# Expert weights of three token blocks added into DRAM by GpSimd's indirect transfers, one-hot products for the fourth

## The reference, cut to what matters

```python
sc = einsum('thcd,hcnd->thcn', q, sub_keys)        # 8 heads, 2 halves, 128 keys each
s1, i1 = top_k(sc[:, :, 0], 16); s2, i2 = top_k(sc[:, :, 1], 16)
top_s, pos = top_k(all 256 sums s1 + s2, 16)       # idx = i1 * 128 + i2 at pos
g = softmax(top_s)                                 # per token and head, over 16
act = gelu(u_tab[idx] @ hb); out = (g * act) @ v_tab[idx]
```

## Time and profile before

| | us |
|---|---|
| runs | 3403.22, 3407.58, 3408.45 (median 3407.58) |
| profiled execution | 3407.45, its span 3405.7 |
| experts: first steps to first one-hot product | 725 to 1292.7 |
| one-hot products | 1292.7 to 1600 |
| SP's first load back of `gd` | 1630.3 |
| GpSimd busy | 439.6 of 3405.7 |

### The profile page before, as it was taken

One profiled execution on the slowest core, in us unless ns is written; L12 is line 12 of the kernel. 1 busy time (PEld: TensorE's weight loads), 2 busy tenths in 40 slices (PEclk: granted clock), 3 DMA queues, 4 the chain that ended last, 5 costly groups with the idle time before them and its releaser, 6 DMA issues.

```text
span 3405.7 us, 37836 instructions
## 1 busy us (share of the span) xinstructions
PE 3253.8 (96%) x14880; PEld 2663.0 (78%) x14880; DVE 1926.9 (57%) x3440; ACT 1232.9 (36%) x1770; POOL 439.6 (13%) x516
## 2 busy tenths in 40 slices
PE   7989999999999999999999999999999977899999
PEld 6767777778888878888788888887888855688887
DVE  5654444567777776665555555555444567544443
ACT  4663444432222235555322222223222233532221
POOL 0000000020000007885000000002000344030000
PEclk9999999899999999999999999999999986799999
DMA  4323111324443445778855555542333310022331
GB/s 139 92 87 100 56 56 56 126 93 129 143 137 126 129 135 158 191 197 204 295 194 195 194 198 198 198 148 75 99 99 99 115 62 13 13 74 99 99 99 62
DMA packets 271199, 424.21 MB, mean 125 GB/s; under 512 B 144816, under 2 KB 148400, under 8 KB 271024
## 3 DMA queue, kind: packets, MB, share of 16 engines
q1 hardware_dynamic: 271024, 421.80, 39.1%
HBM read 348.87 MB, written 72.88 MB: 124 GB/s over the span
## 4 chain that ended last, share of the span: by engine, by line
PE 86%; DVE 7%; ACT 5%; POOL 1%; issue 1%; DMA 1%; SPq 0%; POOLq 0%; ACTq 0%
PE pb L539 27%; PE pb L540 27%; PE pb L541 27%; PE pb L819 3%; ACT scr L1051 2%; DVE S L1486 1%; DVE ST L1494 1%; ACT S L1054 1%; DVE ST L1486 1%; DVE whl L1486 1%; ACT L1051 1%; POOL pad L2018 0%; POOL pad L2015 0%; ACT whl L1054 0%; DVE scr L1494 0%
## 5 line engine op out<-in xcount | busy, mean ns | idle before, releaser
L539 PE MATMUL pb<-H,whl 128*128 128x512 f32 x2416 | 992.2, 411 | 24.2 <-DVE whl L1486 11.6
L540 PE MATMUL pb<-H,whl 128*128 128x512 f32 x2416 | 953.7, 395 | 0.0
L541 PE MATMUL pb<-H,whl 128*128 128x512 f32 x2416 | 953.1, 394 | 0.0
L1486 DVE TENSOR_TENSOR whl<-raw,whl 128x1024 fp32r<-128x1024 f32 (+4 forms) x550 | 649.6, 1195 | 436.8 <-ACT whl L1054 434.7
L1054 ACT ACTIVATE whl<-raw 128x1024 fp32r<-128x1024 f32 (+4 forms) x550 | 543.9, 1003 | 466.2 <-PE pb L541 465.9
L539 PE MATMUL pb<-S,whl 128*128 128x512 f32 (+1 forms) x1716 | 670.2, 391 | 18.8 <-DVE whl L1486 11.7
L540 PE MATMUL pb<-S,whl 128*128 128x512 f32 (+1 forms) x1716 | 667.9, 389 | 0.0
L541 PE MATMUL pb<-S,whl 128*128 128x512 f32 (+1 forms) x1716 | 667.6, 389 | 0.0
L539 PEld LDWEIGHTS pb<-H,whl 128*128 128x128 f32 x2416 | 462.1, 191 | 117.5 <-DVE whl L1486 13.7
L541 PEld LDWEIGHTS pb<-H,whl 128*128 128x128 f32 x2416 | 460.8, 191 | 99.1
L540 PEld LDWEIGHTS pb<-H,whl 128*128 128x128 f32 x2416 | 462.5, 191 | 85.4 <-issue 3.4
(11 more groups left out here) (186 smaller groups left out, 2739.5 us busy)
## 6 DMA issues: line engine op xcount, KB each, us to landing
raw<-in_pu SPq DMA_DIRECT2D x128, 512.0 KB, 3.9
raw<-in_pv SPq DMA_DIRECT2D x128, 512.0 KB, 4.5
raw<-in_w_in SPq DMA_DIRECT2D x72, 512.0 KB, 3.7
ad<-scr SPq DMA_DIRECT2D x128, 256.0 KB, 4.2
gd<-ST SPq DMA_DIRECT2D x8, 4096.0 KB, 21.3
GA<-gd SPq DMA_DIRECT2D x60, 512.0 KB, 4.6
GA<-ad SPq DMA_DIRECT2D x60, 512.0 KB, 6.3
raw<-in_wg SPq DMA_DIRECT2D x44, 512.0 KB, 3.3
```

Of the source, the lines that this page charges most:

```text
L539: e.matmul(o, lh, h, start=start, stop=False, skip_group_check=True)
L540: e.matmul(o, lh, l, start=False, stop=False, skip_group_check=True)
L541: return e.matmul(o, ll, h, start=False, stop=stop, skip_group_check=True)
L1486: return e.tensor_tensor(o, x, y, op)
```

## The change

- Each head is worked one ahead: the query projections (`pq`) and scores (`sk`) of head h+1 stand on TensorE while DVE makes the lists of head h; both have two banks. The low part of a query is a step of its own (`lo`), and on ACT the split of a projection's unit comes behind the query's copy. A head has 64 `u` steps between its parts instead of 80.
- The softmax is made per head: a subtract after `best`, an Exp on ACT of 64 columns, and in `share` the sum, reciprocal, product, and the address (i1 * 128 + i2) * 512 + token.
- SP clears `gd` in the attention with 32 transfers of 1 MB. GpSimd, for token blocks 0 to 2, issues 16 indirect transfers per block and head, each of which adds one number per partition to `gd` in DRAM; a block's transfers of head h wait for those of head h-1.
- Block 3 alone goes through transposes (3), `rows`, `g` (128) and `put` (32). GpSimd builds no one-hot rows. SP's stores take 32 tokens each.
- In the first FFN `sum_of` stands after the second `gate` product.

```diff
@@ peer_order: the order of the choice @@
+    out.append(("pq", 0, 0))
+    u(16)
+    out.append(("sk", 0, 0))
+    out.append(("sk", 0, 1))
     for h in range(8):
         for c in range(2):
-            if (h, c) != (0, 1):
-                out.append(("pq", h, c))
-            u(16)
-            out.append(("sk", h, c))
+            if h < 7:
+                out.append(("pq", h + 1, c))
+            out.append(("top", h, c))
+            if h < 7:
+                out.append(("lo", h + 1, c))
+            u(8 + 8 * c)
+        for c, step in enumerate(("cand", "best")):
+            out.append((step, h))
+            if h < 7:
+                out.append(("sk", h + 1, c))
             u(8)
-        for step in (("cand", h), ("best", h), ("pick", h, 0), ("pick", h, 1)):
-            out.append(step)
+        for c in range(2):
+            out.append(("pick", h, c))
             u(8)
-    out.append(("soft",))
-    u(20)
-    for z in range(3):
-        out.append(("over", z))
-        u(6)
-    left = 8 * (128 - s // 8 - 9)
+        out.append(("share", h))
+        u(8)
+    out.append(("over",))
+    u(8)
+    left = 8 * (116 - s // 8)
     for q in range(3):
         out.append(("rows", q))
-    for q in range(128):
-        if q + 3 < 128:
+    for q in range(32):
+        if q + 3 < 32:
             out.append(("rows", q + 3))
         for k in range(4 * q, 4 * q + 4):
             out.append(("g", k))
             if k % 4 == 3 and q:
                 out.append(("put", q - 1))
-            u((k + 1) * left // 512 - k * left // 512)
-    out.append(("put", 127))
-    u(8 * (124 - s // 8))
+            u((k + 1) * left // 128 - k * left // 128)
+    out.append(("put", 31))
+    u(64)
     out.append(("ga",))
...
@@ build: names @@
+        pq_bank, sk_bank = (2, 6), (3, 7)
+        place = place_t[:, :].rearrange("p (b h k) -> p b h k", b=4, h=8)
...
+        g_rows = gd.rearrange("i p t -> (i p t)").unsqueeze(1)
...
+        def share_of(h):
+            return ST_t[:, 3264 + 64 * (h % 2):3328 + 64 * (h % 2)]
...
@@ tensor: experts @@
-                            q.wait_ge(dve, ("pq", n - 1))
-                            linear(j, bank[2], Hh, Hl, h2, ("pq", n))
+                            q.wait_ge(dve, ("pq", n - 2))
+                            linear(j, bank[pq_bank[c]], Hh, Hl, h2, ("pq", n))
...
-                        q.wait_ge(dve, ("top", n - 1) if n else ("bra", 7))
+                        q.wait_ge(dve, ("top", n - 2) if n > 1 else ("bra", 7))
+                        if n == 1:
+                            q.wait_ge(act, ("rstd", "2"))
...
-                        z = step[1]
-                        if z == 0:
-                            q.wait_ge(act, ("rstd", "2"))
-                        q.wait_ge(dve, "soft")
-                        if z:
-                            q.wait_ge(dve, ("over", z - 1))
-                        for b in range(4):
-                            c = slice(128 * b, 128 * b + 128)
-                            last = e.transpose(bank[6][:, c], (I1, I2, TS)[z][:, c], ident)
-                        last.then_inc(prod.up(("over", z)), 1)
+                        q.wait_ge(dve, ("shared", 7))
+                        for z in range(3):
+                            c = slice(128 * z, 128 * z + 128)
+                            last = e.transpose(bank[6][:, c], (I1, I2, TS)[z][:, 384:512], ident)
+                        last.then_inc(prod.up("over"), 1)
...
-                        elif k == 0:
-                            q.wait_ge(dve, ("top", 15))
-                        if n % 4 < 3:
-                            q.wait_ge(pool, ("hot1", k))
-                        q.wait_ge(dve, ("hot2", k))
-                        last = e.matmul(b[:, c], hot2[n % 4][:, c], hot1[n % 4][:, c], start=True, stop=True, skip_group_check=True)
+                        q.wait_ge(dve, ("hot", k))
+                        last = e.matmul(bank[gbank[n % 4]][:, c], hot2[n % 4][:, c], hot1[n % 4][:, c], start=True, stop=True,
+                                        skip_group_check=True)
...
@@ tensor: ffn @@
-                            two(j, (bank[0], bank[2]), Hh, Hl, hx, (("gate", tag, 0), ("up", tag, 0)), tag)
+                            two(j, (bank[0], bank[2]), Hh, Hl, hx, (("gate", tag, 0), ("up", tag, 0)), tag if tag == "5" else None)
                             continue
                         linear(j, bank[i % 2], Hh, Hl, hx, ("gate", tag, i))
+                        if i == 1 and tag == "3":
+                            sum_of(tag)
...
@@ scalar: experts @@
-                        weights("w_pq", n)
                         if n == 0:
+                            weights("w_pq", 0)
...
-                        copy(qh[c], bank[2]).then_inc(act.up(("pq_hi", n)), 1)
+                        copy(qh[c], bank[pq_bank[c]]).then_inc(act.up(("pq_hi", n)), 1)
+                        weights("w_pq", n)
...
-                    elif what == "soft":
-                        q.wait_ge(dve, "shifted")
-                        run(ACT.Exp, TS, TS).then_inc(act.up("shares"), 1)
...
+                    elif what == "best":
+                        h = step[1]
+                        q.wait_ge(dve, ("shifted", h))
+                        run(ACT.Exp, share_of(h), share_of(h)).then_inc(act.up(("shares", h)), 1)
...
@@ vector: experts @@
+                        weights("sk", 2 * step[1] + step[2])
+                    elif what == "top":
                         h, c = step[1:]
                         n = 2 * h + c
-                        weights("sk", n)
                         q.wait_ge(prod, ("sk", n))
                         for b in range(4):
-                            best16(vals[:, c, b, :], idxu[:, c, b, :], bank[3][:, 128 * b:128 * b + 128], sc2, ("top", n))
+                            best16(vals[:, c, b, :], idxu[:, c, b, :], bank[sk_bank[c]][:, 128 * b:128 * b + 128], sc2, ("top", n))
+                    elif what == "lo":
+                        h, c = step[1:]
+                        n = 2 * h + c
+                        q.wait_ge(act, ("pq_hi", n))
+                        tt(ql[c], bank[pq_bank[c]], f(qh[c]), ALU.subtract).then_inc(dve.up(("pq", n)), 1)
...
+                        soft = share_of(h).rearrange("p (b k) -> p b k", b=4)
+                        tt(soft, TSv[:, :, h, :], TSv[:, :, h, 0:1].to_broadcast([128, 4, 16]), ALU.subtract).then_inc(
+                            dve.up(("shifted", h)), 1)
...
-                    elif what == "soft":
...
+                    elif what == "share":
+                        h = step[1]
+                        top, soft = TSv[:, :, h, :], share_of(h).rearrange("p (b k) -> p b k", b=4)
+                        total, at_ = sm_t[:, 0:4], ST[:, 3392:3456].rearrange("p (b k) -> p b k", b=4)
+                        then(stt(at_, I1v[:, :, h, :], 128.0, I2v[:, :, h, :], ALU.mult, ALU.add))
+                        then(stt(at_, at_, 512.0, tok, ALU.mult, ALU.add))
+                        then(e.tensor_copy(place[:, :, h, :], at_))
+                        q.wait_ge(act, ("shares", h))
+                        then(e.tensor_reduce(total, soft, AX_X, ALU.add))
+                        then(e.reciprocal(total, total))
+                        then(tt(top, soft, total.unsqueeze(2).to_broadcast([128, 4, 16]), ALU.mult), ("shared", h))
                     elif what == "over":
...
                     elif what == "rows":
...
-                        if n % 4 == 3:
-                            tt(o1.rearrange("p (u i) -> p u i", u=4), iota.unsqueeze(1).to_broadcast([128, 4, 128]),
-                               I1[:, 4 * n:4 * n + 4].unsqueeze(2).to_broadcast([128, 4, 128]), ALU.is_equal)
+                        tt(o1.rearrange("p (u i) -> p u i", u=4), iota.unsqueeze(1).to_broadcast([128, 4, 128]),
+                           I1t[:, 4 * n:4 * n + 4].unsqueeze(2).to_broadcast([128, 4, 128]), ALU.is_equal)
                         for k in range(4 * n, 4 * n + 4):
                             c = slice(128 * (k % 4), 128 * (k % 4) + 128)
-                            ts(o2[:, c], iota, I2[:, k:k + 1], ALU.is_equal, TS[:, k:k + 1], ALU.mult).then_inc(
-                                dve.up(("hot2", k)), 1)
+                            ts(o2[:, c], iota, I2t[:, k:k + 1], ALU.is_equal, TSt[:, k:k + 1], ALU.mult).then_inc(
+                                dve.up(("hot", k)), 1)
...
@@ gpsimd @@
-            for n in range(128):
-                if n % 4 < 3:
-                    q.wait_ge(dve, ("over", 2))
-                    if n > 3:
-                        q.wait_ge(prod, ("g", n - 4))
-                    for k in range(4 * n, 4 * n + 4):
-                        c = slice(128 * (k % 4), 128 * (k % 4) + 128)
-                        e.tensor_scalar(hot1[n % 4][:, c], iota, I1[:, k:k + 1], None, ALU.is_equal).then_inc(
-                            pool.up(("hot1", k)), 1)
+            q.wait_ge(zeroed, "cleared")
```

(54 more changed lines are left out.)

40 lines of the change are left out of this document (15 added, 25 removed).

## The result

| | before | after |
|---|---|---|
| median of the runs, us | 3406.59 (3403.22 to 3408.45, 4 runs) | 3327.52 (3326.48 to 3328.51, 4 runs) |
| span of the profiled execution | 3405.7 | 3326.3 |

The ratio is 0.9769 (95% interval 0.9752 to 0.9786): 79 us less. The forecast was 3339 with 3303 to 3410.

The account below looks back on a forecast made before the run. TensorE, busy 96% of the span, was taken as the bound, so work and waits removed from it come off the time. 3407.45 - 88.3 - 1.0 - 6.6 - 8.4 + 23.5 + 10.6 + 2 = 3339 us, range 3303 to 3410.

Parts of the forecast that it names:

- One-hot products, -88.3: One-hot part on TensorE: 384 of 512 products go, at 0.230 us each, saving 88.3 us.
- Softmax, -6.6: The one softmax over all heads goes: TensorE's 4.4 us idle and 2.2 us of slow clock are saved.
- the transposes: Before the one-hot products: nine of twelve go, -1.0 us; the remaining three wait 1.7 us for the last share.
- FFN, -8.4: First FFN: TensorE's 6.2 us wait for GpSimd's sum of squares goes, with its clock loss; 8.4 us saved.
- Heads, +23.5: Expert choice: TensorE idles 2.5 us plus 0.85 of clock in each of seven heads, behind ACT's Exp; 23.5 us added.
- Rival 4: The Exp costs little: DVE runs further ahead, most of 34 us of head stalls go, 3310 us; chance 0.10.
- Head 7, +10.6: Last head: no projection or score left; 6.7 us idle, 2.2 of clock, 1.7 at the transposes; 10.6 us added.
- GpSimd, hidden: GpSimd's 384 indirect transfers, at 1.2 us each, end before SP's loads at about 1570; cost 0.
- rival 1: GpSimd is late: each 0.1 us above 2.0 per transfer adds 38 us; 3530 at 2.5; chance 0.14.
- a tie with 770: GpSimd's transfers: if each holds the queue for its 2.0 us fixed cost, 768 us fill the 770 us window.
- The port, +2: DVE beside GpSimd's transfers: splits stay near 1.225 us, as beside one-input work; 1% more on DVE, +2 us.
- rival 2: The port, slower: GpSimd's transfers hold DVE's operations with two SBUF inputs, +0.62 us each; +80, 3420 us; chance 0.08.

Follow-up runs that it names:

- e3: The kernel after with the first FFN's sum of squares put back into the middle of its first two products: 3334.66 us.
- e1: The kernel after with 2 instead of 16 indirect transfers per block and head, leaving out most softmax weights of blocks 0 to 2: 3322.35 us.
- e5: The kernel after with all four token blocks through GpSimd's transfers (512 instead of 384) and no one-hot products: 3539.62 us.
- e12: The kernel after with one-hot rows made by eight tensor_scalar operations in place of one two-input comparison and four tensor_scalar: 3320.92 us.
- e4: The kernel after without working one head ahead: each head's projections and scores directly before its own lists, 80 u steps a head: 3380.42 us.
- e2: The kernel after with ACT's Exp of a head moved two steps later, from the best lists to the second pick: 3331.39 us.
- e8: The kernel after with Exp at the first pick, the 0 to 127 row read from PSUM, and 8 u steps instead of 16 before the first scores: 3325.37 us.

## Why the prediction was right, point by point

**One-hot products, -88.3.** Right, with a small error: 297.3 us between the first and the last (127 distances) hold 388 steps, 263.8 us; 33.4 / 127 = 0.263 each, where 0.230 was taken. That is +4.2. In the trace of before most products stand in pairs, at 0.229 each, and the 47 that stand alone between three other matmuls cost 0.239, with 0.227 for each of the three; so standing alone explains some 0.01 of the 0.033, and the rest is open.

**Softmax, -6.6.** The wait and its clock loss are gone; neither this nor the transposes was measured apart. **FFN, -8.4.** The wait is gone and nothing is late behind it; e3 prices it at 7.1, and 7.1 is also what the stretch behind the v table's start gained.

**Heads, +23.5.** The mechanism was right, the size three times too large: 58.3 against 57.2 us of work is 1.1 a head (0.44 idle, the rest at restarts), 7.7 for seven. The idle of 2.5 was too long by 2, and the term that was mis-sized is DVE's part of the chain: from ACT's copy of the second projection (928.79) to the table load for the Exp (954.13) are 25.3 us where 27.1 were taken. Nearly all of it is the start: the top list began 1.3 us behind the copy and not 3.0. The clock loss taken behind the idle time did not come at 0.44 us. Rival 4 was half true. **Head 7, +10.6.** 6.6 idle against 6.7, 3.6 us at half clock (1.8) against 2.2; the 1.7 at the transposes did not come. About 8.8 with the restart.

**GpSimd, hidden.** The step that failed. Taken at 1.2 us a transfer, it took 1.975, and the deciding point was put at 2.0 for a window of 770 us: 798 to 1557 us, with SP's loads forecast for 1570, begun at 1558.94. SP would have asked at about 1549, since the heads were shorter than forecast; so rival 1 was true in its mildest form, +4.3 us of idle (8.0 less 3.7), by way of the late `ad` store. Of the 1.975 us 1.84 are the transfer and the gap behind it, and 0.13 are the holds, 50.6 us over all 384. At 1.84 alone, by this sum an estimate, the last would have begun near 1504, 45 us before SP asked: so the price of 1.2 was wrong by 0.64, and it is the holds that made the end late. e1 gives 5.2 with what follows from it. The value between the bounds was chosen by the nearest row, and that row, a compare over 128 partitions, was no kin of a transfer that computes 128 addresses. The Trainium skill (DMA: Bandwidth & Descriptors, "Anatomy of one DMA — SWDGE (gpsimd) path") gives about 2.0 us fixed, mostly the wait for the write's receipt. The size agrees with 1.84 to 1.975 here, but it is held by the issuing engine and does not overlap (e5's 1541 ns and 0.30 behind each), so the reading "a tie with 770" in the prediction was the true one.

**The port, +2.** Zero on that side. DVE's splits beside the transfers, 1220 to 1540 us, for the earlier trace rows:

```profile
L1506 DVE TENSOR_TENSOR whl<-raw,whl x53: 1224/1226/1250, 1223.9 to 1538.4; 128x1024 fp32r<-128x1024 f32 x53
```

The cost lay on the other side: transfers, not DVE's splits, were held, by 25.2 us over 160 of them in this stretch. The prediction let only one-input work of GpSimd's stand for a transfer, since it computes nothing over 512 columns; rival 2 had the contention with DVE's two-input operations right, and the wrong side as the loser. The Trainium skill (SBUF — State Buffer, "Who interferes with whom") says that a DVE instruction with two SBUF inputs contends with a GpSimd one that reads SBUF, and that issue order decides who blocks. The held transfers here agree: one that begins 0.42 us behind a split waits for the split's end (1291.82 to 1294.04). The same section infers that `tensor_tensor` leaves descriptor generation alone; 25.2 us of holds in one stage say that for these indirect transfers it does not. That it names `tensor_scalar` as an operation that can contend agrees with 0.58 us for one at 1298.64 in e12, beside a transfer, where its neighbours take 0.27.

**The 11.5 us to the forecast.** Heads -15.8, head 7 -1.8, port -2.0, the start -0.95 (not forecast), one-hot +4.2, entry +4.3, FFN with the entry's clock +1.3: -10.8; 0.7 are not placed. Errors of 20.6 one way and 9.8 the other made a forecast that looks closer than its parts, and that part of it is luck. By the prediction's own signs the GpSimd step fails outright: it asked for 1 to 1.5 us a transfer and an end ahead of SP's loads, and for idle times of 2 to 3 us a head. What held is the removed work, the removed waits and where the new ones stand.

## To carry to other kernels

Price work that is moved to an idle engine by the rate at which that engine issues it, not by its bytes; where the window and a plausible price are a tie (770 us and 2.0 each), make the tie the first rival and give the move only as many pieces as fit. A function that is not in ACT's loaded table is best put so late in its queue that its input is ready: one line was worth 56 us in e4's order. But once another resource ends last, TensorE's stalls cost nothing, and taking them out earns nothing (e2, e8). A queue that waits for one thing also delays what stands behind it: here the stores of `ad`, and with them a Gelu. Whether these stores on another queue would win back the entry's 5 us was not run.

## What the runs showed that was not expected

- An indirect adding transfer of 128 elements holds GpSimd 1.54 us, and 0.30 pass before the next, with none overlapping (384 and, in e5, 512 in a row).
- One that begins while DVE runs a two-input operation on SBUF waits for its end: up to 2.53 us in e5, 2.56 beside the splits after. How much that costs depends on the distance between the operations: 1575 ns in the mean with splits 5.44 us apart, 1706 with 6.13.
- A head's idle time of 0.44 us leaves TensorE's clock at 1.00, one of 6.6 us is followed by 0.50.
